# Hybrid decoder layer step on one core: three places where work changes its turn in a hand-written order

## The reference, cut to what matters

```python
# mixer
g  = u_val * sigmoid(u_glu);  c = silu(rmsnorm(causal_dwconv(g, 31 taps), conv_norm_g))
xc = causal_dwconv(u_x, 4 taps)
r  = sigmoid(xh @ lru_wa + lru_ba);  i_g = sigmoid(xh @ lru_wx + lru_bx)
a  = exp(-8 * r * softplus(-lru_lambda))
bterm = sqrt(1 - a*a) * (i_g * xc);  h[t] = a[t] * h[t-1] + bterm[t]
yb = h * gelu(u_gelu)
x  = x + rmsnorm(concat[c, yb] @ w_out, post_g)
# second FFN, then the embedding
x    = x + 0.5 * rmsnorm(ffn2(x), ffn2_post_g)
gate = sigmoid(rmsnorm(x, ple_norm_g) @ ple_w_gate)
x    = x + rmsnorm(gate * (p @ ple_w_proj), ple_post_g)
```

## Time and profile before

| | us |
|---|---|
| median of 3 runs (2083.25 to 2094.78) | 2086.84 |
| profiled execution, its own time | 2094.25 |
| its span, first to last instruction | 2092.3 |
| PE busy in the span | 2057.9 (98%) |
| DVE busy | 1182.6 (57%) |
| ACT busy | 679.5 (32%) |
| mean granted TensorE clock | 0.992 |

### The profile page before, as it was taken

The page is one execution under the profiler, slowest core; times in us unless marked ns, Lnnn a source line. Parts: engine busy times, 40 slices in busy tenths (PEclk is TensorE's granted clock), DMA queues, the critical chain, the costliest instruction groups (busy, mean ns, idle before and its releaser), DMA issues. The chain is left out here.

```text
span 2092.3 us, 34476 instructions
## 1 busy us (share of the span) xinstructions
PE 2057.9 (98%) x13041; PEld 2043.9 (98%) x13041; DVE 1182.6 (57%) x2365; ACT 679.5 (32%) x1401; POOL 72.3 (3%) x112
## 2 busy tenths in 40 slices
PE   7999999999999999999999999999999999999998
PEld 7999999999999999999999999999999999999997
DVE  5643555355534579438685765344534454458876
ACT  5321222122222244217684532111221222124555
POOL 0000000000000002330000000000000000000000
PEclk9999999999999999999799999999999999999999
DMA  5180111011101101331121311011101110121212
GB/s 167 61 118 23 60 60 50 10 60 60 58 12 50 60 1 51 75 79 25 41 74 53 98 61 55 16 50 60 60 10 50 60 60 13 47 81 35 68 41 104
DMA packets 153277, 116.17 MB, mean 56 GB/s; under 512 B 72648, under 2 KB 143628, under 8 KB 153200
## 3 DMA queue, kind: packets, MB, share of 16 engines
q1 hardware_dynamic: 117728, 108.41, 16.7%
q10 hardware_dynamic: 33424, 5.67, 2.0%
q0 software_dynamic: 2048, 1.06, 0.3%
HBM read 105.96 MB, written 9.15 MB: 55 GB/s over the span
## 5 line engine op out<-in xcount | busy, mean ns | idle before, releaser
L856 PE MATMUL ps<-x_hi,w_lo 128*128 128x352 f32 x2688 | 887.6, 330 | 8.0 <-DVE x_lo L2175 4.4
L858 PE MATMUL ps<-x_hi,w_hi 128*128 128x352 f32 x2688 | 865.9, 322 | 0.0
L857 PE MATMUL ps<-x_lo,w_hi 128*128 128x352 f32 x2688 | 865.9, 322 | 0.0
L856 PEld LDWEIGHTS ps<-x_hi,w_lo 128*128 128x128 f32 x2688 | 508.6, 189 | 11.2 <-DVE x_lo L2175 5.9
L857 PEld LDWEIGHTS ps<-x_lo,w_hi 128*128 128x128 f32 x2688 | 509.4, 189 | 0.0
L858 PEld LDWEIGHTS ps<-x_hi,w_hi 128*128 128x128 f32 x2688 | 507.0, 189 | 0.0
L856 PE MATMUL ps<-a_hi,wd_lo 128*128 128x352 f32 x1104 | 357.4, 324 | 0.4 <-DVE a_lo L2240 0.4
L857 PE MATMUL ps<-a_lo,wd_hi 128*128 128x352 f32 x1104 | 354.2, 321 | 0.0
L858 PE MATMUL ps<-a_hi,wd_hi 128*128 128x352 f32 x1104 | 354.2, 321 | 0.0
L2288 DVE TENSOR_TENSOR acc<-ps,acc 128x352 f32<-128x352 f32 x480 | 250.3, 523 | 83.8 <-PE ps L858 77.8
L2223 DVE TENSOR_TENSOR tmp_u<-ps,rstd_pre 128x352 f32<-128x352 f32 x132 | 68.9, 524 | 337.0 <-PE ps L858 337.0
(11 more groups left out here) (225 smaller groups left out, 1583.7 us busy)
## 6 DMA issues: line engine op xcount, KB each, us to landing
raw<-in_ffn_w_gu_dram SPq DMA_DIRECT2D x88, 512.0 KB, 3.5
rawd<-in_ffn_w_down_dram SPq DMA_DIRECT2D x22, 1024.0 KB, 7.5
raw<-in_w_in_dram SPq DMA_DIRECT2D x16, 512.0 KB, 3.9
raw<-in_w_out_dram SPq DMA_DIRECT2D x16, 512.0 KB, 3.9
raw<-in_ple_w_gate_dram SPq DMA_DIRECT2D x16, 512.0 KB, 3.5
toeplitz<-rev ACTq DMA_DIRECT2D x8, 512.0 KB, 8.3
x_in<-in_x_prompt_dram SPq DMA_DIRECT2D x4, 512.0 KB, 9.5
toep_first<-toeplitz SPq DMA_DIRECT2D x32, 64.0 KB, 2.2
```

Of the source, the lines that this page charges most:

```text
L856: eng.matmul(dst, wl, xh, start=first, stop=False)
L857: eng.matmul(dst, wh, xl, start=False, stop=False)
L858: return eng.matmul(dst, wh, xh, start=False, stop=last)
```

## The change

The i sigmoid of each row waits for that row's own scan of the pair before. The odd row's gates stand on PE after step k = 2 and no more k = 1, and the convolution parts of that tile begin one step later, two parts at a time from the third step on. Weight unit `mix`+11 is split ahead of chunk 2's `conv_silu` on ACT and ahead of `conv_lo(2)` on DVE, and the wait for `conv_lo` of all chunks goes from output tile (0, 0) to (0, 4). In the gate stage `post3_pair(1, 2)` stands ahead of next_split(1) on DVE, and ACT computes mean("pre4", 1) after four of the eight squares of post3's chunk 2. No instruction is added or taken away but waits.

```diff
 # PE, pair_part
-                    if k == 1:
+                    if k == 2:
                         lru_gates(2 * p - 3)
-                    if slot is not None and k > 1:
-                        conv_part(slot, ((0,), (1,), (2,), (3,), (4, 5), (6, 7))[k - 2])
+                    if slot is not None and k > 2:
+                        conv_part(slot, ((0,), (1,), (2, 3), (4, 5), (6, 7))[k - 3])
 # PE, sixth_unit
-                if (n, k) == (0, 1):
+                if (n, k) == (0, 2):
                     lru_gates(9)
 # ACT, lru_gates
-                        if p and which == "i" and t == 0:
-                            eng.wait_ge(scan_done, 2 * p)
+                        if p and which == "i":
+                            eng.wait_ge(scan_done, 2 * p - 1 + t)
 # ACT
             spread("conv", 2)
+            split_wide(WIDE0["mix"] + 11)
             conv_silu(2)
-            split_wide(WIDE0["mix"] + 11)
 # ACT, oc_copy
                 if (c, m) == (0, 0):
                     eng.wait_ge(psum_free, n)
+                    eng.wait_ge(conv_out[3], 16 * 12)
+                if (c, m) == (0, 4):
                     eng.wait_ge(yc_lo_done, NJ * NC)
-                    eng.wait_ge(conv_out[3], 16 * 12)
 # ACT, gate stage
-            for m in range(KT):
+            for m in range(4):
                 post_square(1, "post3", 2, m)
             mean("pre4", 1)
+            for m in range(4, KT):
+                post_square(1, "post3", 2, m)
             spread("pre4", 1)
 # DVE
             conv_scale(2)
+            split_wide(WIDE0["mix"] + 11)
             conv_lo(2)
-            split_wide(WIDE0["mix"] + 11)
 # DVE, gate stage
             gated(1)
+            post3_pair(1, 2)
             next_split(1)
-            post3_pair(1, 2)
             ple_unit(2)
```

## The result

The kernel after took 2074.68 us (median of 8 runs, 2074.25 to 2076.16), the kernel before beside it 2082.94 (8 runs, 2081.27 to 2094.78). The ratio is 0.9939, interval [0.9915, 0.9963]. A second comparison, made later, gave 2074.69 (11 runs) against 2083.98 (23 runs), ratio 0.9935 [0.9912, 0.9958]. The profiled execution took 2074.45, with a span of 2072.6; PE is busy 2046.5 us of it (99%) and the mean clock is 0.998.

The account below looks back on a forecast made before the run. PE, busy 98% of the span, was taken as the bound, leaving gaps, clock and waits to gain from. 12.4 + 1.1 + 0.65 + 3.6 = 17.75 off 2094.25 gave 2076.5 us, range 2071 to 2089.

Parts of the forecast that it names:

- long stretch of low clock: Convolution parts of one pair, 989.85 to 1016.70: half clock goes once row 7's gap goes, 12.4 us gained.
- part 1, scan wait: Row 7's i gate: PE's 1.50 us wait plus 0.16 of matmul overlap goes, 1.66 us.
- part 1, later step and edges: Gates one step later: r gate waits of 0.41 covered, loop 0.62 us late, two thin edges cost 0.35.
- part 2: Seventh output tile: split fills ACT's idle time, so oc_copy and PE come 0.65 us earlier.
- short fall at the output tile: Second clock fall, 1090 to 1100: kept because a gap of 1.8 us stays, so nothing gained.
- part 3: Gate stage, unit 4: waits for x_lo (2.5 us) and the norm (1.1 us) go, 3.6 in all.
- row 9's r gate as a thin edge: At full clock, row 9's r gate would meet an r sigmoid about 0.1 to 0.3 us late.
- The other edge, row 11's r gate: Row 11's r gate would wait about 0.3 us for row 10's r sigmoid, the chain being 0.48 later.
- my price of the six gate matmuls at full clock: Six gate matmuls after the slow convolution parts: 1.90 us against 0.96 at full clock, 0.94 gained.
- The rival with the fall all the same: Clock still falls in the convolution stretch, giving 2089 us; chance 0.2.
- the one with an earlier fall: Moved waits bring the fall forward to 969.7, ahead of the fourth pair, giving 2103.5 us; chance 0.06.
- ple+3 or at pair 3: Gate-stage rival: ple+3 or pair 3's x_lo late, 3 us of 3.6 lost, 2079.5; chance 0.08.

Follow-up runs that it names:

- before at full clock: The unedited kernel before, profiled once more; its profile holds no fall of the clock, though both gaps are there: 2082.98 us.
- the run with the scan wait alone: Kernel before with each i sigmoid waiting for its own row's scan, gates still behind step k = 1: 2082.29 us, ratio 0.9981.
- the run with the gap put back: Kernel after with eight tiny ACT operations ahead of row 6's i sigmoid, its waits and order kept: 2076.50 us, ratio 0.9947.
- the old scan wait: Kernel after with one wait of the even row's i sigmoid for both scans put back, gates one step later: 2076.54 us, ratio 0.9971.
- part 2 alone: Kernel before with only weight unit mix+11 split ahead of chunk 2's SiLUs and conv_lo(2), the wait moved to tile 4: ratio 1.0010.
- the longer gap: Kernel before with six tiny ACT operations between the scan and row 6's i sigmoid: ratio 1.0042.

## Why the prediction was right or wrong

The forecast of 2076.5 for the time of the new kernel was 1.8 us above its median, 2.05 above its profiled execution, and inside its own range of 2071 to 2081. It got there because it starts from an execution that held the long stretch and takes the stretch off. What was wrong is the size of the change: 17.75 us, of which 8.3 were measured between the medians. The small terms were wrong in size as well, every one of them too low. By the same points of the timelines:

| term | predicted | measured | from |
|---|---|---|---|
| long stretch of low clock | 12.4 | 11.6 | row 11's i gate at 98.96 us from the first gate in the profile of before, 87.40 in before at full clock |
| part 1, scan wait | 1.66 | 1.83 | 87.40 less 85.57 in the run with the scan wait alone |
| part 1, later step and edges | -0.56 | 0.45 | 85.57 less 85.12 after |
| part 2 | 0.65 | 0.9 to 1.0 | gap 2.46 to 1.46; from the first gate, the seventh tile is 14.75 earlier, of which 13.84 by row 11's i gate |
| short fall at the output tile | 0 | 1.5 | from the seventh tile to the next norm sum: 1095.29 to 1107.43 before, 12.14; 1080.91 to 1091.51 after, 10.60 |
| part 3 | 3.6 | 4.0 | 1984.49 to 1964.63, 19.86, less 15.86 at the stage's start |

**The failing step** is the clock term of part 1: 12.4 us put into the gain in full on the strength of one profiled execution, as if the kernel before always held the long stretch. I saw that "the median before may hold the stretch in part or not at all", and counted it all the same. The runs show it in 24 of 99, so it is worth 11.6 us to those and nothing to the median. Three runs with a median of 2086.84 said little of this; the kernel before is a 2083.0 kernel that is at 2095 in a quarter of its runs. Against its usual run the change gains 8.3 us, where my terms without the long stretch gave 5.35. The timelines add up to 8.7 (1.83 + 0.45 + 0.95 + 1.5 + 4.0), and the 1.5 of the short fall is in four of six profiles with the old gap only; before at full clock has none. I drew the border of a clear gain 0.5% under that median of three; the kernel after repeats within 0.1% (2074.25 to 2076.16), and so its gain is clear though it is only 0.4% by the medians.

**Part 1, the wait.** Right: 1.50 us of idle went, ACT's i sigmoid of row 6 starts at 986.69 (I said near 986.6), and row 7's at 988.80 (988.7). One detail differs: I had row 4's scan done long before, at 985.95; it ends at 986.66 now and is what the sigmoid waits for.

**Part 1, the later step.** Wrong in sign. I let the loop be 0.62 late by the fourth pair; it was 0.51 late at row 4's gates (31.84 us from the first gate, against 31.33 in before at full clock) and then gained, 0.33 late at row 6's (45.84 against 45.51). Taking the r gate's wait away in each pair was worth a little more than the delay of DVE's chain: against the run with the scan wait alone, row 8's gates come 0.23 earlier. And I had row 9's r gate as a thin edge that might cost; at full clock it waited 0.25 already, and the step took that away, worth 0.49 up to row 10's gates. The profile of before could not show it: in the low stretch PE came late enough for ACT. The other edge, row 11's r gate, gave way about as I said: from row 10's last gate to row 11's i gate takes 0.27 longer than with the scan wait alone. The waits at xc_lo are as predicted, 0.45 to 0.60.

**Part 1, the clock.** The stretch did go, in every run. The 12.4 was too high by 0.8. Half of that is my price of the six gate matmuls at full clock, 0.96: in before once more they take 1.37 (1004.64 to 1006.01), so the low clock adds 0.53 and not 0.94. The other half is row 9's r gate, whose wait of 0.25 the usual run pays and the low one doesn't. The rival with the fall all the same (0.2) and the one with an earlier fall (0.06) did not come: with waits of 0.4 to 0.6 at the even rows' gates, none of the 44 runs of the kernels that have them and no gap at row 7 holds the long stretch. As for the rule in the Trainium skill (TensorE: Matmul & The Clock Gate, Why this matters for your kernels), which warns only of clearly longer gaps: the runs don't bear out that shorter ones are safe. With 1.5 us of idle the clock fell for long in a quarter of the runs, with no gap in none.

**Part 2.** The mechanism held: oc_copy waits behind the SiLUs still, 1.46 is left where I said near 1.8. The raw half came in time, so ACT's split and SiLUs stand without a break at 1074.47. I kept the second fall because a gap stayed. It went. Six profiles with a gap of 1.4 to 1.8 at this tile show no fall after it; of six with 2.3 to 2.8, four show one. That suggests that the length of this gap matters too, but twelve profiles don't show it. Where the fall comes it costs 1.5 us: 12.14 from the tile to the next norm sum in before, 10.58 in before at full clock, which has the same gap and no fall.

**Part 3.** Both gaps went, and no new wait came in at ple+3 or at pair 3. In the stage's own time x_lo of pair 3 came 3.2 us earlier (1975.76 to 1956.72, less 15.86) where I had 2.75, and it ends 0.6 us ahead of PE's 1958.23.

**Open.** What makes one gap in four into a long stretch, and why it ends where the next full tiles begin, no run here settles. Nor does one settle whether the later step or the 0.24 us ahead of row 7's r gate matters besides the gap. The 2 of 24 against 35 of 123 hints at it, but it rests on the run with the gap put back (0 of 12, before beside it 6 of 16); with the old scan wait the rate was before's own (2 of 12, 3 of 18). The run that would tell, a longer gap with the gates after k = 2, was not made. What is shown is that without the gap there is no long stretch (0 of 63), and that twice the gap brings it in 10 of 12.

## What to carry to other kernels

When a profile shows a stretch of low clock, count it first over many runs of the same kernel, by the list of their times and clocks: a profiled execution is one draw, and a term that stands in a quarter of the runs is worth its full size to those and nothing to the median. Then size the direct waits against a profile without the stretch, since the slow stretch hides waits that the usual run pays. Here a wait of PE of 1.5 us just ahead of many small matmuls was worth taking away for more than its length.

## What was not expected of the hardware

A fall of the clock differs from run to run of one kernel: the same gap of 1.5 us has none after it, a short one (0.85 over 10 us) or one of some 27 us at 0.50 (989.85 to 1016.70 in the earlier trace rows), which costs 11 to 12 us (medians 2092.60 against 2081.33 in part 2 alone, 2096.91 against 2085.27 with the longer gap). The length of the gap moves the odds: 24 of 99 at 1.5, 10 of 12 at 2.97. Another section of the Trainium skill (TensorE: Matmul & The Clock Gate, A second HAM failure mode: psum-queue depth-cycling) does tell of a kernel in which frequent short idles between groups of matmuls were enough to swing the clock. The runs here agree in so far as the gap ahead of the stretch was short, 1.5 us; it was one gap, not many. And a gap that ACT's small operations made, of 1.42 us, brought no long stretch in 12 runs of 12.
